# Second block's convolution moved from VectorE to GpSimd, the index's projections first, masks at their own widths

## The reference, cut to what matters

```python
z = rmsnorm(x, mix_norm) @ w_in
(aq, ak, av, iq, ik, iw, bq, bk, bv, bg, br, cu, dcq, dckv, dkpe) = jnp.split(z, ...)
y_a = dsa_mixer(aq, ak, av, iq, ik, iw, ...)   # attention on keys that an index picks
y_b = gla_mixer(bq, bk, bv, bg, br, ...)       # gated linear attention
y_c = conv_mixer(cu, c_dw_w, c_dw_b, c_norm)   # causal depthwise convolution
y_d = mla_mixer(dcq, dckv, dkpe, ...)          # attention on low-rank keys

def conv_mixer(u, w_dw, b_dw, g_norm):
    a, gate = jnp.split(u, 2, axis=-1)
    h = a * jax.nn.sigmoid(gate)
    h = depthwise convolution of h with 31 taps over time, padded on the left, + b_dw
    return jax.nn.silu(rmsnorm(h, g_norm))
```

## Time and profile before

| what | value |
|---|---|
| time, median of 3 runs (lowest, highest) | 4692.57 us (4691.49, 4697.6) |
| the profiled execution: time, span | 4690.48 us, 4689.0 us |
| busy in the span: TensorE, VectorE, ScalarE, GpSimd | 4133.8, 2447.1, 1351.7, 24.6 us |
| mean granted TensorE clock | 0.919 |
| first layer's mixer in the span | about 2540 to 2980 us |
| second layer's mixer in the span | about 3800 to 4245 us |

### The profile page before, as it was taken

One profiled execution on the slowest core, in us unless ns is written; L12 is line 12 of the kernel. 1 busy time (PEld: TensorE's weight loads), 2 busy tenths in 40 slices (PEclk: granted clock), 3 DMA queues, 4 the chain that ended last, 5 costly groups with the idle time before them and its releaser, 6 DMA issues.

```text
span 4689.0 us, 46819 instructions
## 1 busy us (share of the span) xinstructions
PE 4133.8 (88%) x19069; PEld 3239.9 (69%) x19069; DVE 2447.1 (52%) x3968; ACT 1351.7 (29%) x2067; POOL 24.6 (1%) x40
## 2 busy tenths in 40 slices
PE   7347999999999999998999765899999987579999
PEld 6345888666677888887877554788778775357877
DVE  3773788777734444443332876433233239764331
ACT  3124322333333333332222222322132232223221
POOL 0000000000000000000000000000000000000000
PEclk9568999999999999998999876899999998768999
DMA  3001245455566666652332110133322321101232
GB/s 94 9 1 45 81 134 142 150 180 180 179 196 188 188 186 188 195 177 75 95 97 74 54 56 0 41 94 95 99 72 95 96 71 41 51 1 59 94 99 68
DMA packets 253286, 473.52 MB, mean 101 GB/s; under 512 B 15808, under 2 KB 138848, under 8 KB 250896
## 3 DMA queue, kind: packets, MB, share of 16 engines
q1 hardware_dynamic: 253072, 470.53, 33.0%
HBM read 399.95 MB, written 70.52 MB: 100 GB/s over the span
## 4 chain that ended last, share of the span: by engine, by line
PE 77%; DVE 17%; ACT 4%; issue 1%; DMA 0%; POOL 0%; DVEq 0%; ACTq 0%; SPq 0%; POOLq 0%
PE ps L353 23%; PE ps L355 22%; PE ps L354 22%; DVE arena L1111 2%; PE ps L456 2%; DVE arena L1718 2%; DVE arena L2568 1%; DVE st L2566 1%; PE ps L2117 1%; PE ps L2093 1%; DVE arena L2485 1%; DVE wtwo L344 1%; DVE arena L1714 1%; DVE arena L1715 1%; PE ps L1567 1%
## 5 line engine op out<-in xcount | busy, mean ns | idle before, releaser
L344 DVE TENSOR_TENSOR wtwo<-wraw,wtwo 128x1024 fp32r<-128x1024 f32 x416 | 507.8, 1224 | 828.9 <-ACT wtwo L334 828.6
L353 PE MATMUL ps<-XH,wtwo 128*128 128x512 f32 (+1 forms) x1928 | 790.6, 410 | 2.6 <-DVE wtwo L344 2.6
L355 PE MATMUL ps<-XH,wtwo 128*128 128x512 f32 (+1 forms) x1928 | 759.8, 394 | 0.0
L354 PE MATMUL ps<-XL,wtwo 128*128 128x512 f32 (+1 forms) x1928 | 759.5, 394 | 0.0
L334 ACT ACTIVATE wtwo<-wraw 128x1024 fp32r<-128x1024 f32 x416 | 437.8, 1056 | 463.1 <-PE ps L355 442.3
L344 DVE TENSOR_TENSOR wlast<-wraw,wlast 128x1024 fp32r<-128x1024 f32 x202 | 246.8, 1224 | 427.4 <-ACT wlast L334 427.2
L355 PEld LDWEIGHTS ps<-XH,wtwo 128*128 128x128 f32 x1928 | 363.2, 188 | 86.6
L353 PEld LDWEIGHTS ps<-XH,wtwo 128*128 128x128 f32 x1928 | 364.2, 189 | 76.0 <-issue 5.4
L354 PEld LDWEIGHTS ps<-XL,wtwo 128*128 128x128 f32 x1928 | 364.7, 189 | 70.3
L353 PE MATMUL ps<-XH,wlast 128*128 128x512 f32 x920 | 379.7, 413 | 2.6 <-DVE wlast L344 2.6
L355 PE MATMUL ps<-XH,wlast 128*128 128x512 f32 x920 | 364.8, 397 | 0.0
(11 more groups left out here) (418 smaller groups left out, 6548.0 us busy)
## 6 DMA issues: line engine op xcount, KB each, us to landing
wraw<-in_ut SPq DMA_DIRECT2D x128, 512.0 KB, 4.2
wraw<-in_v SPq DMA_DIRECT2D x128, 512.0 KB, 4.1
wraw<-in_ffn_gate SPq DMA_DIRECT2D x88, 512.0 KB, 3.5
wraw<-in_ffn_up SPq DMA_DIRECT2D x88, 512.0 KB, 3.5
wraw<-in_ffn_down SPq DMA_DIRECT2D x88, 512.0 KB, 3.5
acts<-arena SPq DMA_DIRECT2D x128, 256.0 KB, 4.5
gates<-arena SPq DMA_DIRECT2D x16, 2048.0 KB, 9.1
arena<-gates SPq DMA_DIRECT2D x32, 1024.0 KB, 7.9
```

The source lines that it names most:

```text
L344: ve.e.tensor_tensor(W.items[n][8], W.rawof(n), W.items[n][7], ALU.subtract).then_inc(*ve.up("wlo", n))
L353: mm(out, lh, rh, start=start, stop=False)
L354: mm(out, lh, rl, start=False, stop=False)
L355: return mm(out, ll, rh, start=False, stop=stop)
```

## The change

The convolution's arithmetic goes from VectorE to GpSimd (`po_conv`), as a copy of the bias, then for each tap a product with the weight, broadcast over 512 columns, into HT, and a sum into YC, each waiting for the one before. It stands in GpSimd's queue ahead of `po_b`. It forms H there too. The norm of the convolution moves to the second half as stream `c`, four steps, from the gated part's step 40 on. The index's projections come first in the plan, the loads and all engines' lists; the index may start after three projections, and a round is `pxxxxxxh`. The diagonal mask of the scores becomes an add of `CM` on VectorE. MB moves into a part of the first block's memory and is made at the start of `po_ssm`; M has its own width for each query block. ScalarE and VectorE wait for H before the second half.

```diff
@@ First
-        ar = k.level(4096 + 2112)
-        self.MT, self.XC = ar(8, 512), ar(16, 132)
+        ar = k.level(4096 + 2112 + 272)
+        self.MT, self.XC, self.MB = ar(8, 512), ar(16, 132), ar(272)
@@ def po_ssm(self):
+        g, MB = po.e, self.MB
+        g.memset(MB, 0.0).then_inc(*po.up())
+        po.after().affine_select(out=MB[:, 0:128], in_=MB[:, 0:128], compare_op=ALU.is_gt, fill=NEG,
+                                 base=0, pattern=[[1, 128]], channel_multiplier=-1)
+        g.affine_select(out=MB[:, 128:256], in_=MB[:, 128:256], compare_op=ALU.is_ge, fill=NEG,
+                        base=0, pattern=[[-1, 128]], channel_multiplier=1).then_inc(*po.up("masks"))
         k.begin(po, "in", "pe", "ac", "ve")
@@ class Mixer:
-        self.M = ar(4, 512)
+        Mm = ar(1152)
+        self.M = [k.CM[:, 384:512], Mm[:, 0:256], Mm[:, 256:640], Mm[:, 640:1152]]
+        self.H, self.HT = ar(2, 544), ar(512)
+        self.csq, self.crs = self.H[:, :, 0:512], self.HT
...
@@ def order1(self):
-        steps = {"p": 18, "c": 17, "x": 3 * 13 + 1, "h": 2}
-        needs = {"c": 4, "x": 7, "h": 8}
+        steps = {"p": 18, "x": 3 * 13 + 1, "h": 2}
+        needs = {"x": 3, "h": 8}
...
-            for b in "pxxxcxxxh":
+            for b in "pxxxxxxh":
@@ def ac_proj1(self):
+        for m in range(4):
+            even(m, ("cu", l, m), self.CU[:, m])
+            if m == 3:
+                for j in range(2):
+                    ac.wait_ge(*at("pj", ("cu", l, 2 + j)))
+                    ac.after().activation(self.CU[:, 2 + j, :], self.CU[:, 2 + j, :],
+                                          ACT.Sigmoid).then_inc(*ac.up("cgate", l, j))
+            yield
+    def po_conv(self):
+        k, po, at, l = self.k, self.k.po, self.k.at, self.l
+        g, H, HT, YC = po.e, self.H, self.HT, self.YC
+        k.begin(po, self.before)
+        g.memset(H[:, :, 0:32], 0.0).then_inc(*po.up())
+        for m in range(2):
+            po.wait_ge(*at("pj", ("cu", l, m)))
+            po.wait_ge(*at("cgate", l, m))
+            po.after().tensor_tensor(H[:, m, 32:544], self.CU[:, m, :], self.CU[:, 2 + m, :],
+                                     ALU.mult).then_inc(*po.up())
+        po.note("ch", l)
+        for m in range(2):
+            y = YC[:, m, :]
+            po.after().tensor_copy(y, k.col(f"cb{l}", m).broadcast_to([128, 512])).then_inc(*po.up())
+            for j in range(31):
+                wc = k.col(f"cw{l}", 31 * m + j).broadcast_to([128, 512])
+                po.after().tensor_tensor(HT, H[:, m, 2 + j:2 + j + 512], wc, ALU.mult).then_inc(*po.up())
+                po.after().tensor_tensor(y, y, HT, ALU.add).then_inc(*po.up())
+        po.note("conv", l)
@@ def ac_conv(self):
         ac.wait_ge(*at("conv", l))
-        a(self.csq, self.AC, ACT.Square).then_inc(*ac.up("csq", l))
+        a(self.csq, self.YC, ACT.Square).then_inc(*ac.up("csq", l))
+        yield
+        yield
         ac.wait_ge(*at("cvar", l))
         a(self.crs, self.crs, ACT.Sqrt).then_inc(*ac.up("csd", l))
+        yield
@@ def ve_conv(self):
-        for j in range(31):
-            for m in range(2):
...
-                    v.scalar_tensor_tensor(self.AC[:, m, :], src, wc, self.AC[:, m, :], ALU.mult,
-                                           ALU.add).then_inc(*ve.up("ct", l, j, m))
-            if j % 2 or j == 30:
-                yield
-        ve.note("conv", l)
+        yield
+        ve.wait_ge(*at("conv", l))
         ve.wait_ge(*at("css", l))
@@ def ve_index(self):
-            ve.wait_ge(*at("causal", l, i))
+            ve.after().tensor_tensor(s[:, nk - 128:nk], s[:, nk - 128:nk], k.CM[:, 384:512], ALU.add).then_inc(*ve.up())
@@ def order2(self):
-        steps = {"a": self.n_a, "d": self.n_d, "b": self.n_b, "x": self.left}
+        steps = {"a": self.n_a, "d": self.n_d, "b": self.n_b, "c": 4, "x": self.left}
...
+                if b == "c" and done["b"] < 40:
+                    continue
@@ def ve(self):  (and ac)
         k.begin(k.ve, ("mix1", l))
-        self.merged2({"a": self.ve_a(), "d": self.ve_d(), "b": self.ve_b()}, x)
+        k.ve.wait_ge(*k.at("ch", l))
+        self.merged2({"a": self.ve_a(), "d": self.ve_d(), "b": self.ve_b(), "c": self.ve_conv()}, x)
@@ def po(self):
-        self.po_index()
+        self.po_conv()
         self.po_b()
```

More of the change, by code:

```diff
@@ L2275, in order1 @@
     def order1(self):
-        steps = {"p": 18, "c": 17, "x": 3 * 13 + 1, "h": 2}
-        needs = {"c": 4, "x": 7, "h": 8}
+        steps = {"p": 18, "x": 3 * 13 + 1, "h": 2}
+        needs = {"x": 3, "h": 8}
         done = dict.fromkeys(steps, 0)
         out = []
-        while any(done[b] < steps[b] for b in "pch"):
-            for b in "pxxxcxxxh":
+        while any(done[b] < steps[b] for b in "ph"):
+            for b in "pxxxxxxh":
                 if done[b] < steps[b] and done["p"] >= needs.get(b, 0):
@@ L2291, in merged1 @@
             next(gens[b], None)
-        for b in "pch":
+        for b in "ph":
             assert next(gens[b], "end") == "end", b
@@ L2305, in pe_proj1 @@
         yield
+        for m in range(4):
+            pe_proj(k, ("cu", l, m), XH, XL, 0, 5)
+            yield
         pe_tok(k, ("aqk", l), 512, XH, XL, AT4, 0, 5)
@@ L2420, in ve_proj1 @@
         yield
+        for m in range(4):
+            odd(m, ("cu", l, m), self.CU[:, m])
+            yield
         splits(k, split_ve, ("aqk", l), 512)
@@ L2468, in ve_conv @@
         k, ve, v, at, l = self.k, self.k.ve, self.k.ve.e, self.k.at, self.l
[L2469 to L2474, removed]
-        for j in range(31):
[L2476 to L2481, removed]
-                                    ALU.add).then_inc(*ve.up("ct", l, j, m))
-                else:
-                    ve.wait_ge(*at("ct", l, j - 1, m))
-                    v.scalar_tensor_tensor(self.AC[:, m, :], src, wc, self.AC[:, m, :], ALU.mult,
-                                           ALU.add).then_inc(*ve.up("ct", l, j, m))
-            if j % 2 or j == 30:
-                yield
-        ve.note("conv", l)
+        yield
+        ve.wait_ge(*at("conv", l))
         ve.wait_ge(*at("css", l))
@@ L2531, in ac_index @@
                 yield
-    def po_index(self):
-        k, po, at, l = self.k, self.k.po, self.k.at, self.l
-        for i in range(1, 4):
-            nk = 128 * (i + 1)
-            po.wait_ge(*at("sc", l, i, 7))
-            po.e.affine_select(out=self.SCO[:, nk - 128:nk], in_=self.SCO[:, nk - 128:nk], compare_op=ALU.is_ge,
-                               fill=NEG, base=0, pattern=[[-1, 128]],
-                               channel_multiplier=1).then_inc(*po.up("causal", l, i))
     def ve_index(self):
@@ L3108, in sp @@
         k, l = self.k, self.l
-        for m in range(4):
-            load(k, ("cu", l, m))
         for m in range(2):
@@ L3113, in sp @@
         load(k, ("ik", l))
+        for m in range(4):
+            load(k, ("cu", l, m))
         splits(k, load, ("aqk", l), 512)
```

64 lines of the change are left out of this document (24 added, 40 removed).

## The result

| | before | after |
|---|---|---|
| time, median (lowest, highest) | 4692.03 us (4690.27, 4697.6) | 4741.72 us (4741.07, 4746.34) |
| ratio, 95% interval | | 1.0106 (1.0093 to 1.0118) |
| the profiled execution's span | 4689.0 us | 4740.1 us |
| busy: TensorE, VectorE, ScalarE, GpSimd | 4133.8, 2447.1, 1351.7, 24.6 us | 4158.7, 2444.6, 1356.4, 370.2 us |
| mean granted TensorE clock | 0.919 | 0.913 |

The change makes the kernel slower by 49.7 us; the forecast was 4755, 13 us above. Lines of code go by their number in the kernel before; in a view of after or of an experiment the same line has another number (L2963 is L2968 in after, L344 is L343, and L2728 is L2733). The first line to read is VectorE's busy time. Over 120 instructions of 0.744 us, some 90 us, left it, and it is as busy as before (2444.6 against 2447.1). Something gives the time back.

The account below looks back on a forecast made before the run. The prediction took TensorE to bound the front half, then L2963's wait for GpSimd's chain: 26 + 23 us late, plus 2 x 7 for the moved norm, +63 on 4692.6 gives 4755 us; 8-in-10 range 4650 to 4835.

Parts of the forecast that it names:

- rival (3): VectorE pays 66 us for the port shared with GpSimd, 12 more a layer: 4779 us, chance 0.12.
- The index earlier: Mixer's front half: four channel projections no longer precede the index; first score at 2580.9 instead of 2603.0 us.
- The prize: After the front half, everything would begin 28 us earlier: VectorE at L2963 at 2790 instead of 2817.9 us.
- the 94 us of TensorE's work from 2649: Front half: query/key weights' matmuls and seven projections, 22.1 + 33.5 + 38.5 us, done at 2743 instead of 2761.
- Instruction lengths on GpSimd: Convolution chain: 1.09 us per product or sum plus 0.14 between them, 156.6 us a layer undisturbed.
- The port: VectorE and GpSimd hold each other at SBUF: 49 us added to GpSimd's chain, 33 to 66 us to VectorE.
- What is late next: At L2963 VectorE waits for GpSimd's memset of QX behind the convolution: 26 us later, 23 in the second layer.
- The tail, moved: Convolution's norm, now in the second half near L3003: costs between 0 and 14.5 us, taken as 7 per layer.
- Edits at nothing: Mask MB, constants, causal adds on VectorE, waits on H and weight-load order: counted as no change.
- The sum: 26 + 23 + 2 x 7 = +63 us on the median of 4692.6: 4755 us.
- Rival (1): GpSimd is in time and the kernel faster: 4657 us with no port held, 4651 with one-pass instructions; chance 0.25.
- The tells: Signs: VectorE splits above 1.22 us with MAX8 at 0.70; long VectorE idle before L2963, ended by memset near 2844.

Follow-up runs that it names:

- The writes: Kernel after with the taps left out and four GpSimd memsets per tap, which read nothing, in their place: 4691.26 us, ratio 0.9993 to before.
- Late head norms: Kernel after with the taps left out and the head norms allowed to start after 12 projections instead of 8: 4675.73 us, ratio 0.9954 to before.
- e5_order_alone: Kernel before with only the order changed: index projections first, convolution on VectorE from projection 7, its norm ending the first half: 4700.6 us, ratio 1.0009.

## Why the prediction was right, and where its reasons were wrong

**The sign and nearly the size came out, by another wait than the one it named.** What I put as the likeliest was the chain of L2963's wait for GpSimd; what happened is the mechanism that rival (3) named, VectorE's own delay, and cheaper than its 4779. That the number lies within 13 us is luck in part: the delay at L2963 came out 25 us smaller than forecast over the two layers, and the tails with the later start of the mixer 11 us larger.

- *The index earlier.* The first score was to come at 2580.9, 40.4 behind the mixer's start; it came at 41.1. GpSimd's input was to be there 96.0 behind it, and its second product for H began at 97.9. Right.
- *The prize.* Failed. L2963 was to come 28 us earlier but for GpSimd; with the taps left out it comes 14.8 earlier. The step that failed is the 94 us of TensorE's work from 2649, by which I let TensorE run without a stop at full clock. In the kernel without taps it starts 2.6 later, is busy 99.1 us, 5.1 more, at a mean granted clock of 0.95, and idles 5.2: 12.9 of the 13.2 that are missing. One thing that the step had left out is ScalarE's queue: the search, pulled forward, pushes against the head norms, and a head norm's root stands ahead of the next weights. Late head norms give back 6.7, with TensorE idle for 0.8 instead of 5.2 and the clock at 0.98. The other is TensorE's own work: with late norms the same 553 instructions are still busy 96.8 us, at nearly full clock, so 2.8 of the 5.1 is work that the 94 missed and 2.3 goes with the clock.
- *Instruction lengths on GpSimd.* Two reads one after another, 1.09 us, and a hand-over of 0.14, 2.46 a tap. Measured: 1.04 and 1.26 and 0.08, 2.46 a tap. The sum of a tap is right, its parts are not: a product with a broadcast column is shorter than a sum of two full inputs. The chain takes 181 us (2643.2 to 2824.3).
- *The port.* Mechanism right, split between the engines wrong. 49 us were to be added to the chain; 62 x 2.46 and two copies are 154, so 27 were. VectorE was to pay 33 to 66 us for 60 instructions; it is 38.9, for 60. The Trainium skill (SBUF — State Buffer, Summary: rules for kernel authors) lets the second to issue block until the first is done, and the two places above agree, either way round. The same page (Who interferes with whom) says that a VectorE instruction with two SBUF inputs meets only a GpSimd one that reads SBUF, not one that only writes. The writes agree: 1224 ns a split.
- *What is late next.* Failed, and the forecast rested on it. With the chain at 2824 instead of 2842, and VectorE at L2963 at 2834.4 instead of 2790 plus 33, the chain was 8.2 us early. Both errors act in the same direction: the chain was held less, and VectorE was 13 us later than reckoned before any holding. The prize that I missed and the wait that I overrated nearly cancel at L2963: 13.1 / 11.2 us late, where 26 / 23 were forecast.
- *The tail, moved.* 7 a layer, of 0 to 14.5. With the taps left out, L2963 to the output projection takes 169.6 against 158.1: 11.5, inside the bounds, and a term of the sum that was too small. In after it is 10.5 and 11.0. The norm with its four table loads is 6.8 and 10.8 of it; the 3.7 left in the first layer go with the granted clock, as shown above.
- *Edits at nothing.* The adds of the diagonal mask are not at fault: the third score comes within 0.2 us of 104.1 in the kernels without taps and in those of the order alone, which keep GpSimd's selects. But something among the edits is not free: from 1465 to 2099 us after and every kernel made from it lose 3.9 us, the kernels made from before lose none, and after's mixer starts 3.5 later. The prediction put all edits outside the mixer at nothing; which of them it is stays open.
- *The sum.* 13.1 + 11.2 at L2963, 10.5 + 11.0 behind it, and a mixer that starts 3.5 us later, make 49.3 of the 51.1 between the two profiled spans.
- *Rival (1)* is nearly what the writes show: the two-input instructions aren't held, only a few scalar forms are, and GpSimd is in time. It was priced at 4657 and measures 4691. Even had the port been free, the change would have gained nothing that can be told (the interval without taps is 0.998 to 0.9999), so the chance of 0.25 for faster rested on a prize that wasn't there.
- *The tells.* Splits above 1.22 us with MAX8 at 0.70: seen. A long idle of VectorE ended by the memset near 2844: not seen. The text's own criterion for (3), VectorE at L2963 later than the memset, doesn't decide: the copy ahead of L2963, held by the memset, takes 0.62 us and ends with it, in before and after alike. What points to (3) is that the memset itself had waited 8.20 us for ScalarE, and that for VectorE.

## What to carry to other kernels

Work handed to GpSimd isn't free for VectorE if its instructions read SBUF: reckon for each VectorE instruction with two SBUF inputs, and each copy or scalar form of doubled rate however small, about half a GpSimd instruction (in this kernel 0.65 us for each of some 60), and look whether what VectorE does meanwhile is on the path. Price an offload with two kernels before it is tuned: one that leaves the work out, which shows the whole prize, and one with writes of the same length, which parts the port from the queue. And when one stream is pulled forward, follow what stands behind its late waits in the in-order queue of a third engine, here the weights behind a root on ScalarE.

## What the runs showed of the hardware

- GpSimd, float32, 128x512, each waiting for the one before (after): 1.04 us for a product with a broadcast column, 1.26 for a sum of two tiles, 1.27 for a product of two tiles (L2460), 0.53 for a memset, 0.08 between them.
- Among instructions that meet at the port, who starts first decides: four scans of 128x128 go from 405 to 1292 ns each and a 128x16 scalar form from 174 to 992, while the scans of 128x512 and 128x384 at L2582, each ahead of a sum by a little, keep their 1224 and 957 ns.
- The hold is mutual and uneven: in the first layer of after some 27 us on GpSimd's 126 chained instructions, 38.9 on some 60 of VectorE's.
- GpSimd's writes do hold VectorE's scalar forms of doubled rate (477 to 826 ns) and a copy of 128x128 from SBUF to SBUF (0.22 to 0.62 us under QX's memset), and not forms with two inputs (splits 1224 ns).
- The same 448 TensorE instructions of the mixer's second half are busy 99.3 us at a mean granted clock of 0.62 and 104.2 at 0.58, and the stretch takes 3.7 us longer (e5_order_alone, its two layers).
